# A linear-recurrence stage dissolved into the last stage of a hybrid decoder step: 16 chunk steps between attention slots, 24 in an expert pipeline, and a row ring of 11 in place of 13

## What is computed

```python
def hgrn_chunk(S, q, k, log_f, v):
    G = jnp.cumsum(log_f, axis=2)
    decay = jnp.exp(jnp.where(causal, diff, -jnp.inf))      # diff[t,s] = G[t] - G[s]
    scores = jnp.einsum('bhtk,bhsk,bhtsk->bhts', q, k, decay)
    o = (jnp.einsum('bhts,bhsv->bhtv', scores, v)
         + jnp.einsum('bhtk,bhkv->bhtv', q * jnp.exp(G), S))
    S_new = (jnp.exp(G_last[:, :, 0, :, None]) * S
             + jnp.einsum('bhsk,bhsv->bhkv', k * jnp.exp(G_last - G), v))
    return o, S_new

def peer_block(h, w_pq, sub_keys, expert_u, expert_v):
    ...                                    # queries, scores, top 16 of 16 x 16 pairs -> e, gate
    act = gelu(einsum('nd,nhkd->nhk', h, expert_u[e]))
    return einsum('nhk,nhkd->nd', gate * act, expert_v[e])
```

## Time and profile before

| | us |
| --- | --- |
| median of three runs | 4478.01 |
| lowest and highest run | 4467.41, 4478.89 |
| the profiled execution, its own time | 4464.47 |
| span of the profiled execution, first to last instruction | 4462.8 |
| hgrn_steps within the span | 766 to 1016 |
| first block's attention slots | 1044.9 to 1092.8 |
| expert pipeline, step 0 to the end | 1171 to 4463 |

### The profile page before, as it was taken

How to read it: one execution, slowest core, us unless ns; L and a number is a source line. 1 busy time by engine, 2 the same in 40 slices (tenths; PEclk the granted TensorE clock), 3 DMA queues, 4 the chain that set the end, 5 groups by cost and what they waited for, 6 DMA issues and landing times.

```text
span 4462.8 us, 44080 instructions
## 1 busy us (share of the span) xinstructions
PE 2978.8 (67%) x12880; PEld 1617.8 (36%) x12880; DVE 2941.4 (66%) x7334; ACT 861.1 (19%) x1870; POOL 2358.5 (53%) x2200
## 2 busy tenths in 40 slices
PE   5878776994785687884568787875666643344434
PEld 3546555662542353441234443441233321111111
DVE  6577851222467748787675687786778785777775
ACT  1433110112232013341111233331111100000000
POOL 1010110000247746677576667777677775777775
PEclk8989888665766887787778768777788776677767
DMA  6575973223569988889899989999899998999998
GB/s 237 188 311 226 392 297 99 52 53 110 208 239 373 344 311 311 333 327 375 312 371 340 351 325 357 362 345 388 321 392 407 404 386 296 367 407 401 381 404 347
DMA packets 432909, 1389.10 MB, mean 311 GB/s; under 512 B 67174, under 2 KB 135014, under 8 KB 420382
## 3 DMA queue, kind: packets, MB, share of 16 engines
q0 software_dynamic: 306432, 1216.48, 71.0%
q1 hardware_dynamic: 102094, 144.95, 9.6%
q10 hardware_dynamic: 24144, 24.86, 1.6%
HBM read 1333.57 MB, written 56.86 MB: 312 GB/s over the span
## 4 chain that ended last, share of the span: by engine, by line
PE 22%; POOL 17%; DVE 13%; issue 10%; DMA 9%; DVEq 2%; ACT 2%; SPq 1%; ACTq 1%; PEld 0%; POOLq 0%; PEldq 0%
POOL st_rows L1465 17%; DMA st_rows<-in_peer_u,st_expert 6%; PE st_ps_q L1750 4%; PE st_ps_y L1801 3%; PE st_ps_m L1674 3%; DVE st_rows L2026 3%; PE st_ps_s L1786 2%; PE st_ps_q L1721 2%; PE st_ps_m L1698 2%; PE st_ps_t L1707 1%; PE st_ps_m L1727 1%; DMA st_gate<-scr_proj 1%; DMA st_rows<-in_peer_v,st_expert_v 1%; PE st_ps_s L1765 1%; DVE st_diag L1989 1%
## 5 line engine op out<-in xcount | busy, mean ns | idle before, releaser
L1465 POOL DMA_INDIRECT st_rows<-in_peer_v,st_expert_v x1024 | 1097.2, 1071 | 623.3 <-issue 290.2
L1465 POOL DMA_INDIRECT st_rows<-in_peer_u,st_expert x1024 | 1154.4, 1127 | 512.5 <-issue 311.8
L2026 DVE CUSTOM_DVE_ANT_0 st_rows<-st_rows,st_h 128x1024 f32<-128x1024 f32 x1024 | 1225.5, 1222 | 254.9 <-DMA st_rows<-in_peer_u,st_expert 233.3
L1801 PE MATMUL st_ps_y<-st_rows,st_diag 128*32 128x512 f32 x4096 | 899.0, 744 | 209.8 <-DMA st_rows<-in_peer_v,st_expert_v 115.0
L1786 PE MATMUL st_ps_s<-st_weight,st_pick_tokens 128*128 128x16 f32 x512 | 115.0, 364 | 613.0 <-DVEq L2084 613.0
L1801 PEld LDWEIGHTS st_ps_y<-st_rows,st_diag 128*32 128x32 f32 x4096 | 193.2, 130 | 861.9 <-DMA st_rows<-in_peer_v,st_expert_v 432.6
L1786 PEld LDWEIGHTS st_ps_s<-st_weight,st_pick_tokens 128*128 128x128 f32 x512 | 108.1, 312 | 620.3 <-DVEq L2084 620.3
L606 PE MATMUL pd_ps<-pd_w,pd_xnT 128*128 128x256 f32 x1152 | 271.8, 395 | 26.6 <-ACT pd_stage L515 13.8
L1750 PE MATMUL st_ps_q<-st_shared 128*128 128x128 f32 (+3 forms) x1024 | 250.6, 408 | 10.3 <-issue 7.0
L606 PEld LDWEIGHTS pd_ps<-pd_w,pd_xnT 128*128 128x128 f32 x1152 | 225.5, 199 | 70.1 <-issue 38.6
L1970 DVE TENSOR_TENSOR st_spread<-st_ps_s,st_own_slot 128x64 f32<-128x64 f32 x128 | 28.7, 224 | 330.6 <-PE st_ps_s L1778 202.9
(11 more groups left out here) (313 smaller groups left out, 4325.2 us busy)
## 6 DMA issues: line engine op xcount, KB each, us to landing
st_shared<-in_w_pq_heads SPq DMA_DIRECT2D x32, 1024.0 KB, 8.2
st_rows<-in_peer_u,st_expert POOLq DMA_INDIRECT x1024, 7.8
st_rows<-in_peer_v,st_expert_v POOLq DMA_INDIRECT x1024, 7.7
pd_w<-in_w_in SPq DMA_DIRECT2D x14, 1024.0 KB, 12.2
scr_proj<-pd_stage ACTq DMA_DIRECT2D x8, 1152.0 KB, 22.1
hs_step<-scr_factors SPq DMA_DIRECT2D x40, 208.0 KB
scr_score<-st_sc_out ACTq DMA_DIRECT2D x64, 130.0 KB
st_sc<-scr_score SPq DMA_DIRECT2D x64, 130.0 KB, 6.5
```

Of the source, the lines that this page charges most:

```text
L1465: pool.indirect_dma_start(rows[n % R][:, :], None, src, bass.IndirectOffsetOnAxis(ap=idx, axis=0)).then_inc(row_loaded[n % R], 16)
L1801: ins = nc.tensor.matmul(ps_y[j * QUAD:(j + 1) * QUAD, c * 512:(c + 1) * 512], diag[k % 2][:, QS * j + q, :], rows[n % R][:, c * 512:(c + ...
L2026: nc.vector.tensor_tensor_reduce(out=rows[n % R][:, :], in0=rows[n % R][:, :], in1=hb, scale=1.0, scalar=0.0, op0=ALU.mult, op1=ALU.add, a ...
```

## The change

hgrn_steps is gone; its 40 chunk steps stand in stream. Sixteen of them (EARLY_CHUNKS) are spread over the 22 slots of block 0's attention; chunks 16 to 39 stand one each in steps 0 to 23 of the pipeline (CHUNK_AT). To make room in SBUF the ring has 11 rows in place of 13, and y is written over h, so that y and the semaphore h_used go. The factors have two buffers in place of four, and are loaded two chunks ahead by ScalarE's queue, once the outputs of the chunk two before are done. kn, v, scores and output rows of both buffers share three tiles by partition offsets.

In PSUM the early chunks borrow ps_s (turned rows, scores) and ps_y (kv, outputs), which are free before the pipeline; the later ones borrow ps_q[0] (turned rows, scores, outputs) and ps_q[1] (kv), which attention and score_head also use. So in a step with a chunk, TensorE does outputs_of(c) first, and before it starts attention slots or score_head it waits for S_ready and oc_read of this chunk (VectorE's decays-and-adds, ScalarE's copy); within(c+1) stands behind them, in front of spread_experts. VectorE does the decays-and-adds (carry_state) behind the second dot in steps with attention, behind the fifth in the others, and the mask behind route. GpSimd makes a few more constants.

```diff
-R_TILES = 13
+R_TILES = 11
+EARLY_CHUNKS = 16
...
+    FIRST_SLOTS = range(-ATT_LEAD, len(TILES[0]) + ATT_TRAIL)
+    EARLY_AT = {t: EARLY_CHUNKS * n // len(FIRST_SLOTS) for n, t in enumerate(FIRST_SLOTS)
+                if EARLY_CHUNKS * (n + 1) // len(FIRST_SLOTS) > EARLY_CHUNKS * n // len(FIRST_SLOTS)}
+    CHUNK_AT = {c - EARLY_CHUNKS: c for c in range(EARLY_CHUNKS, N_CHUNK)}
...
+        turned_bank = lambda c: ps_s if early(c) else ps_q[0]
+        kv_bank = lambda c: ps_y[:, 0:512] if early(c) else ps_q[1][:, :]
+        out_bank = lambda c: ps_y[:, 512:1024] if early(c) else ps_q[0][:, :]
...
+            def chunk_rows(c):
+
+                act.wait_ge(oc_ready, c + 1)
+                if c + 2 < N_CHUNK:
+                    load_chunk(act, c + 2)
+                if c >= 2:
+                    act.wait_ge(oc_stored[c % 2], 16 * (c // 2))
+                nc.scalar.copy(o_c[c % 2], out_bank(c)[0:C, :])
+                act.drain().then_inc(oc_read, 1)
+                act.dma_start(o_hg[c * C:(c + 1) * C, :], o_c[c % 2]).then_inc(oc_stored[c % 2], 16)
...
+            def within(c):
+
+                bank = turned_bank(c)
+                pe.wait_ge(step_loaded[c % 2], 32 * (c // 2 + 1))
+                if c > 0:
+                    pe.wait_ge(kn_ready, c)
+                    pe.wait_ge(score_ready, c)
+                if not early(c):
+                    pe.wait_ge(oc_read, c)
+                    if scores_issued["n"] > 0:
+                        pe.wait_ge(z_ready, scores_issued["n"])
+                for h in range(HH):
+                    ins = nc.tensor.transpose(bank[0:C, h * HG_D:(h + 1) * HG_D], step[c % 2][:, h, KE, :], ident[:, :])
+                ins.then_inc(k_turned, 1)
...
             for k in range(STEPS):
+                if k in CHUNK_AT:
+                    outputs_of(CHUNK_AT[k])
                 if k in TURN:
                     turn(TURN[k])
                 if k in MIX:
                     mix(MIX[k])
+                if k in CHUNK_AT and (k in ATTEND or k in SCORE):
+                    pe.wait_ge(S_ready, CHUNK_AT[k] + 1)
+                    pe.wait_ge(oc_read, CHUNK_AT[k] + 1)
                 for g, t in ATTEND.get(k, ()):
                     attend(g, t)
                 for g, hd in SCORE.get(k, ()):
                     score_head(g, hd, k)
+                if k + 1 in CHUNK_AT:
+                    within(CHUNK_AT[k + 1])
                 if k + 1 < STEPS:
                     spread_experts(k + 1)
...
                 for s in range(K):
                     dot(row_u(k, s), h[b % 2][:, :], act_in[k % 2][:, s:s + 1])
+                    if k in CHUNK_AT and s == (1 if slots else 4):
+                        carry_state(CHUNK_AT[k])
...
-    stages = (project_and_decode, hgrn_steps, stream)
+    stages = (project_and_decode, stream)
```

More of the change, by code:

```diff
@@ L1442, in _ @@
                                         pattern=[[1, P]], channel_multiplier=-1)
+            pool.drain()
+            for u in range(2):
+                nc.gpsimd.affine_select(out=causal[32 * u:32 * u + C, :, :], in_=causal[32 * u:32 * u + C, :, :], compare_op=ALU.is_ge, fill=0.0,
+                                        base=0, pattern=[[0, HH], [1, C]], channel_multiplier=-1)
+                pool.drain()
             nc.gpsimd.memset(pick_tokens[:, :, :], 0.0)
@@ L1825, in _ @@
             pe.wait_ge(keys_ready, 1)
-            for t in range(-ATT_LEAD, len(TILES[0]) + ATT_TRAIL):
+            within(0)
+            for t in FIRST_SLOTS:
                 attend(0, t)
+                if t in EARLY_AT:
+                    if EARLY_AT[t] + 1 < EARLY_CHUNKS:
+                        within(EARLY_AT[t] + 1)
+                    outputs_of(EARLY_AT[t])
             mix(0)
@@ L2117, in _ @@
             dve.drain().then_inc(keys_centred, 1)
-            for t in range(-ATT_LEAD, len(TILES[0]) + ATT_TRAIL):
+            dve.wait_ge(decay_loaded, 16)
+            mask(0)
+            for t in FIRST_SLOTS:
                 attend(0, t)
+                if t in EARLY_AT:
+                    if EARLY_AT[t] + 1 < EARLY_CHUNKS:
+                        mask(EARLY_AT[t] + 1)
+                    carry_state(EARLY_AT[t])
             dve.wait_ge(w_out_loaded, 32)
```

239 lines of the change are left out of this document (99 added, 140 removed).

## The result

The changed kernel takes 4535.44 us (median of 4 runs, 4511.21 to 4543.92) where the kernel before takes 4478.45: 1.0125 times as long, 95% interval 1.0093 to 1.0157. I had predicted 4540. The profiled execution has a span of 4542.2 us, 79.4 more than the one of before. That is 22 more than the 57 between the medians: the profiled execution of the changed kernel was the slowest of its four, that of the kernel before was under its median (4464.5 against 4478).

The account below looks back on a forecast made before the run. Recurrence bound by TensorE; expert pipeline by a loop through GpSimd's row issues, VectorE's dots and TensorE, no engine full. -250 + 2 + 130 + 60 + 57 + 12 + 58 = +69, 4533, median put at 4540 us; range 4435 to 4630.

Parts of the forecast that it names:

- The stage: The recurrence's own stage, hgrn_steps, from its first load to the last stage's first instruction, goes: -250 us.
- the early slots: Sixteen chunks between the first block's attention slots: 178 us in place of 48, so +130.
- The clock term: TensorE's granted clock in the first block's slots: a mixture near the low end, 0.50, giving loops of 10.4 us.
- The first gather: Sign of being right: the first gather comes near 1053 us.
- Chunks in steps: Chunks 16 to 39, one each in steps 0 to 23 of the expert pipeline: +129 us.
- attention steps: Steps 0 to 2 and 8 to 14: a chunk costs about 6 us in each of ten, +60.
- score steps: Steps 6, 7, 20 to 23: scores wait for carry_state, 8 us on average, plus 1.5 for within: +57.
- The ring: Expert pipeline with 11 row buffers, not 13: u rows issued 2.5 us later where first dots wait, +58 us.
- A: Rival: the recurrence finds cover under idle TensorE and the kernel gets faster, 4407, median 4415; chance 0.16.
- B: Rival: gains and costs cancel within 0.3%, 4461 to 4478 us; chance 0.08.
- C: Rival: each of GpSimd's 54 waits for a v row costs two issues, 135 us, not 58; 4610; chance 0.19.
- D: Rival: no overlap, each of 24 chunks adds its 6.2 us and 3.3 of load, 228 not 129; 4640; chance 0.07.

Follow-up runs that it names:

- before_again: The kernel before, unchanged, run and traced a second time: 4468.44 us, on a chip of the first kind.
- ring9: The kernel before with 9 row buffers in place of 13: 4656.02 us beside 4474.12, ratio 1.0415, first kind of chip.
- early_rows: The changed kernel with the 16 early chunks' factors and v in unused row buffers, loaded four chunks ahead: 4804.51 us, ratio 1.0049 to the kernel before.
- no_carry: The changed kernel without VectorE's four decays-and-adds in steps 0 to 23, waits kept: ratio 1.0109 to the kernel before, first kind of chip.
- ring11: The kernel before with 11 row buffers in place of 13, nothing else changed: 4797.26 us beside 4778.17, ratio 1.0027, second kind of chip.
- after_again: The changed kernel itself, measured again on a chip of the second kind: 4841.54 us beside 4835.02 for the kernel before, ratio 1.0037.
- ring11_b: The kernel before with 11 row buffers in place of 13, measured again: 4813.39 us beside 4835.02, ratio 0.9972, second kind of chip.

## Why the prediction held, and which terms did not

**The stage (-250), the constants (+2), the early slots (+130).** As predicted: -250.6, +1.6, +129.0. The 250 belongs to one execution, though: in before_again hgrn_steps takes 239.9 us and in ring9 248.0, so the total is good to some 10 us at best. The clock term was the choice that mattered: I took a mixture near 0.50, and it was 0.50. (TensorE was 95% busy in the recurrence, 233.5 of 246.4 us, not 96.) The sign that TensorE waits about 1 us per chunk for factors was right in kind, though only 8.3 us are named over the 16. My picture of the loop, the slot hidden behind the load, was wrong in part: early_rows shows that without the load wait the slot's matmuls come into the open, and a loop falls from 10.1 to 9.3, not to 7.9.

**The first gather (1053) and the first dot.** The gather was at 1053.24. From there to the first dot it took 15.8 us longer than before, and no term had it: I read the steps' waits and not the two lines ahead of the loop over steps, where mask(16) waits for a matmul behind all scores. The prediction priced what the change adds inside steps, and this addition stands ahead of them.

**Chunks in steps (+129).** With the ring equal on both sides, 120 to 123 us on the second kind of chip, and by ratio 139 with the first dot in it. By kind of step only steps 3 to 7 are firm (24 predicted, 26.9 and 27.8 measured); the attention steps (60) measure 59 or 43 by the choice of pair, score steps 20 to 23 (38) 21 or 35. On the first kind, with the ring, the score steps are dear (56.9), of which about 26 are the later start of the scores; which part of the rest is within's, the ring's or something else is open. The mechanism of score steps, that the scores wait for the decays behind the fifth dot, is in the trace, and step 20 came out as predicted: 7 us predicted, 6.9 measured. Its size was too high elsewhere: step 21 has 6.9 where I had 9.5, as its first dot no longer comes 2 us behind the end of values, and the delay grew by 1 in step 6 where I had 4, so on average over the six steps it is 5.7, where I took 8. I had given VectorE 31 of the 129 by its own work and more by waits; no_carry puts its decays at 20, and the waits by line say that TensorE is what attention steps wait for.

**The ring (+58).** Too high. In steps 24 to 63, where nothing else differs that costs time, it is 18 to 25 us, not 33. GpSimd's waits became more there (45 against 30 to 32), and a row's landing time fell by 1.2 us in the median; that the queue in front of the DMA engines drained further than the 0.2 us per step that I let it absorb fits both, but no run shows the queue itself. The count behind the 33 and 25 was off by a little: of the 36 first dots, 15 and not 13 lie in steps 26 to 48, and 12 and not 14 behind them, which would have made the term 62. In steps 0 to 23 VectorE's whole wait for u rows did not grow (76.8 to 70.3), but the part at the first dots, which is what my 25 was about, grew by 21. How much of this is a loss of its own and how much only moved there from later dots is open: if the parts stand as in ring9 (71 to 114), the ring is about 12 of the 159, by the first dots up to 21, and the chunks take the rest, 138 to 147. ring11 never ran on the first kind of chip, so this division is an estimate. The Trainium skill's rule on consistent bubbles (Perfetto Trace Analysis, section Optimization Strategy), that a repeating gap can mean too few buffers, would by my reading have had the upper end, 135. From 13 to 11 rows that price is not reached; from 13 to 9 it would be 54 x 5 = 270, and +182 was measured.

So the total of 4540 beside 4535 owes something to luck: by these estimates the ring was some 15 to 24 too high and the chunk steps on this kind of chip some 9 to 18 too low, 16 before the first dot were missing, and the medians stand 57 apart where the traces stand 79 apart.

**The rivals.** A (faster) needed a clock above 0.7 in the early slots; it was 0.50, and 0.53 in early_rows. B's mechanism, that things cancel, is what the second kind of chip shows: 1.0037, interval 0.9983 to 1.0092. There the rows come slower, and the ring's term is nothing. On one chip, after_again against ring11_b, the sum can be read: the first dot comes 103 us earlier and steps 0 to 23 take 105 us longer. C fell with the late steps, where it had 32 waits x 2.5 = 80, D with early slots of 177 and chunks of about 5 to 6 us.
